# First mixer's attention taken in pairs of heads, with selection, norm and lift woven into it

## The reference, cut to what matters

```
def dsa_attention(q, k, v_lat, iq, ik, iw, w_uv):      # 8 heads of 64, top 128 keys
        dots = jnp.einsum('bqhe,bse->bqhs', iqb, ik)
        score = jnp.einsum('bqh,bqhs->bqs', iwb, jax.nn.relu(dots))
        score = jnp.where(mask, score, -jnp.inf)
        _, sel = lax.top_k(score, top_k)
...
        prob = jax.nn.softmax(logits, axis=-1)
        o_lat = jnp.einsum('bhqk,bqkl->bqhl', prob, v_sel)
        return jnp.einsum('bqhl,hld->bqhd', o_lat, w_uv)    # the lift
def diff_attention(q, k, v, lam, subln_g, lam_init):   # 4 heads, two maps each
        prob = jax.nn.softmax(jnp.where(mask, s, -jnp.inf), axis=-1)
        a = prob[0] - lam * prob[1]
...
    return rms_norm(o, subln_g) * (1.0 - lam_init)      # the heads' norm
def even_mixer(...):
    return jnp.concatenate([a_out, b_out], axis=-1) @ w_out
```

## Time and profile before

| what | before |
|---|---|
| median of 3 runs | 3308.28 us |
| lowest, highest | 3301.98, 3309.21 us |
| profiled execution, its own time | 3297.97 us |
| its span, first to last instruction | 3296.6 us |
| TensorE busy | 3149.0 us, 96% of the span |
| VectorE, ScalarE, GpSimd busy | 1364.8, 1168.3, 1147.7 us |
| mean granted TensorE clock | 0.968 |
| chain that ended last, TensorE's share | 84% |

### The profile page before, as it was taken

How to read it: one execution, slowest core, us unless ns; L and a number is a source line. 1 busy time by engine, 2 the same in 40 slices (tenths; PEclk the granted TensorE clock), 3 DMA queues, 4 the chain that set the end, 5 groups by cost and what they waited for, 6 DMA issues and landing times.

```text
span 3296.6 us, 36185 instructions
## 1 busy us (share of the span) xinstructions
PE 3149.0 (96%) x14236; PEld 2514.4 (76%) x14236; DVE 1364.8 (41%) x2455; ACT 1168.3 (35%) x2028; POOL 1147.7 (35%) x480
## 2 busy tenths in 40 slices
PE   8999998989999999999989999989999989999998
PEld 6888776668888878887758888867758768876786
DVE  5311496844121451113964321367153423156442
ACT  4222464333222442223414232344323432345422
POOL 4444431014444444444414444433314332300143
PEclk9999998799999999999999999999999999979999
DMA  4333221003333323332303333333213334300032
GB/s 141 102 96 97 81 83 39 1 26 102 96 98 98 93 89 96 98 98 89 102 21 114 97 96 101 95 97 108 86 38 97 99 104 159 96 1 1 20 96 76
DMA packets 76524, 274.33 MB, mean 83 GB/s; under 512 B 8472, under 2 KB 9368, under 8 KB 75973
## 3 DMA queue, kind: packets, MB, share of 16 engines
q1 hardware_dynamic: 76356, 272.03, 26.6%
HBM read 269.85 MB, written 2.15 MB: 83 GB/s over the span
## 4 chain that ended last, share of the span: by engine, by line
PE 84%; DVE 11%; ACT 2%; issue 2%; POOL 1%; DMA 0%; SPq 0%; ACTq 0%; DVEq 0%; POOLq 0%
PE ps L480 23%; PE ps L481 23%; PE ps L482 23%; PE ps L1479 5%; PE ps L1453 4%; DVE arena L2101 3%; PE ps L1467 1%; PE ps L1465 1%; DVE arena L1735 1%; PE ps L2671 1%; PE ps L2533 1%; POOL w_lo L455 0%; ACT w_hi L432 0%; PE ps L2484 0%; DVE arena L1724 0%
## 5 line engine op out<-in xcount | busy, mean ns | idle before, releaser
L455 POOL TENSOR_TENSOR w_lo<-ring,w_hi 128x1024 fp32r<-128x1024 f32 x463 | 1131.9, 2447 | 2123.9 <-ACT w_hi L432 2082.4
L480 PE MATMUL ps<-x_hi,w_hi 128*128 128x512 f32 x2168 | 860.3, 397 | 34.2 <-POOL w_lo L455 21.1
L481 PE MATMUL ps<-x_lo,w_hi 128*128 128x512 f32 x2168 | 849.4, 392 | 0.0
L482 PE MATMUL ps<-x_hi,w_lo 128*128 128x512 f32 x2168 | 849.1, 392 | 0.0
L432 ACT CAST w_hi<-ring 128x1024 fp32r<-128x1024 f32 x473 | 493.9, 1046 | 746.7 <-PE ps L482 741.8
L480 PEld LDWEIGHTS ps<-x_hi,w_hi 128*128 128x128 f32 x2168 | 410.7, 189 | 128.4 <-issue 19.6
L481 PEld LDWEIGHTS ps<-x_lo,w_hi 128*128 128x128 f32 x2168 | 410.6, 189 | 88.6 <-issue 4.4
L482 PEld LDWEIGHTS ps<-x_hi,w_lo 128*128 128x128 f32 x2168 | 410.4, 189 | 86.6
L480 PE MATMUL ps<-r_hi,w_hi 128*128 128x512 f32 x1120 | 437.4, 391 | 11.5 <-issue 11.5
L481 PE MATMUL ps<-r_lo,w_hi 128*128 128x512 f32 x1120 | 436.7, 390 | 0.0
L482 PE MATMUL ps<-r_hi,w_lo 128*128 128x512 f32 x1120 | 436.5, 390 | 0.0
(11 more groups left out here) (240 smaller groups left out, 3311.5 us busy)
## 6 DMA issues: line engine op xcount, KB each, us to landing
ring<-in_stream SPq DMA_DIRECT2D x473, 512.0 KB, 3.5
arena<-in_cmp_w SPq DMA_DIRECT2D x16, 512.0 KB, 4.5
arena<-frev SPq DMA_DIRECT2D x1, 3072.0 KB, 14.8
h<-in_x SPq DMA_DIRECT2D x4, 512.0 KB, 7.1
out<-arena SPq DMA_DIRECT2D x4, 512.0 KB
arena<-in_p SPq DMA_DIRECT2D x2, 512.0 KB
arena<-in_mem SPq DMA_DIRECT2D x1, 1024.0 KB
arena<-in_pool_recip SPq DMA_DIRECT2D x1, 1024.0 KB
```

The source lines that it names most:

```text
L455: self.nc.gpsimd.tensor_tensor(self.w_lo[:, n % SPLIT, :], self.ring[:, n % RING, :], self.w_hi[:, n % SPLIT, :].bitcast(F32), ALU.subtrac ...
L480: nc.tensor.matmul(out, a[0], b[0], start=start, stop=False)
L481: nc.tensor.matmul(out, a[0], b[1], start=False, stop=False)
L482: return nc.tensor.matmul(out, a[1], b[0], start=False, stop=stop)
```

## The change

`attention` is no longer used by the first mixer. In its place:

- A new function `paired_attention` takes 32 pairs: the two maps of a differential head, or two neighbouring sparse heads. The two score products of a pair lie in the upper and the lower 64 rows and follow each other directly. Its rounds are `scores(it)`, `turn(it-2)`, `values(it-4)` on TensorE; `store(it-5)` (of differential pairs), `invert(it-1)`, `bias(it)` and selection on VectorE; `store(it-5)` (of sparse pairs), `scale(it-1)`, `exponentials(it)`, `copy(it-3)` on ScalarE.
- PSUM: two banks for each of two pairs of scores, two banks for one turned pair, one bank for the output. A `turn` waits for the copy of the pair before.
- The diagonal matrices are made by ScalarE (`scale`) in place of VectorE, and one copy takes both turned units of a pair.
- The weighing of the index products moves from a stage of its own into the generator `select_keys`.
- The heads' norm (`SubNorm`) is woven into rounds 21 to 28: its sums are taken with tokens on partitions, 16 products of one column, so that root and reciprocal work on 128x16; the factors are spread back by ScalarE and a product with ones.
- The lift (`Lift`) goes by query tile, eight products of 128 columns at the end of rounds 29, 30, 32 and 36.
- `ev_out` takes its tiles in the order 4 to 7, 0 to 3, and its first two tiles are rounded at the end of the attention.

```diff
+EV_ROWS = (4, 5, 6, 7, 0, 1, 2, 3)
...
-        @block.vector
-        def _(dve):
-            k.vlink(nc.vector.tensor_copy(scores[:, 0, 0:P], k.c("chunkmask")[:, SEQ - P:SEQ]))
-            for i in range(1, TT):
-                w = P * (i + 1)
...
+def select_keys(k, dve, dots, cut, iw, scores, top):
...
+        w = P * (i + 1)
+        work = scores[:, i, 0:w]
+        for h in range(4):
+            dve.wait_ge(*cut[i, h])
+            wt = iw[:, i, h:h + 1]
+            if h == 0:
+                k.vlink(nc.vector.tensor_scalar(work, dots[i][:, h, :], wt, None, ALU.mult))
+            else:
+                k.vlink(nc.vector.scalar_tensor_tensor(work, dots[i][:, h, :], wt, work, ALU.mult, ALU.add))
+            yield i, w
+        k.vlink(nc.vector.tensor_tensor(work, work, k.c("chunkmask")[:, SEQ - w:SEQ], ALU.subtract))
+        yield i, w
         for _ in range(TOPK // 8):
             k.vlink(nc.vector.max(top, work))
             k.vlink(nc.vector.match_replace(work, top, work, gone))
...
+def paired_attention(k, pairs, scratch, turned_at, gate, steps, lift, subln, rows):
...
+            def scores(p):
+                u = pairs[p]
+                if p >= 2:
+                    pe.wait_ge(biased.handle, biased.at(2 * p - 2))
+                for j in range(2):
+                    b = 2 * (p % 2) + j
+                    if p < 2:
+                        k.bank(pe, b)
+                    ins = nc.tensor.matmul(k.ps[:, b, 0:u.w], u.q[j], u.key[j], start=True, stop=True)
+                ins.then_inc(scored.handle, 1)
+            def turn(p):
+                u = pairs[p]
+                pe.wait_ge(diag.handle, diag.at(p + 1))
+                if p >= 1:
+                    pe.wait_ge(copied.handle, copied.at(p))
+                for j in range(2):
+                    if p == 0:
+                        k.bank(pe, 4 + j)
+                    for t in range(u.i + 1):
+                        ins = nc.tensor.matmul(k.ps[:, 4 + j, t * P:(t + 1) * P], ex[p % 3][:, j, t * P:(t + 1) * P],
+                                               dg[p % 2][:, j, :], start=True, stop=True)
+                ins.then_inc(turned.handle, 1)
...
+            for it in range(n + 6):
+                if it < n:
+                    scores(it)
+                if 2 <= it < n + 2:
+                    turn(it - 2)
+                if 4 <= it < n + 4:
+                    values(it - 4)
+                subln.pe(pe, it - norm_at)
+                if it in lift_at:
+                    lift.pe(pe, lift_at[it], stored.token(last[lift_at[it]] + 1))
...
+            def bias(p):
+                u = pairs[p]
+                dve.wait_ge(scored.handle, scored.at(p + 1))
+                if p >= 3:
+                    dve.wait_ge(turned.handle, turned.at(p - 2))
+                for j in range(2):
+                    nc.vector.tensor_tensor_reduce(ex[p % 3][:, j, 0:u.w], k.ps[:, 2 * (p % 2) + j, 0:u.w], u.bias, 1.0, 3e38,
+                                                   ALU.add, ALU.min, low[:, p % 3, j:j + 1]).then_inc(biased.handle, 1)
...
+            work = steps(dve)
+            spent = 0
+            due = [weight[p] / weight[needed[TT - 1] - 1] for p in range(n)]
+            upto = np.cumsum([0] + [(5 + 2 * (TOPK // 8) + 1) * P * (i + 1) for i in range(1, TT)])
+            for it in range(n + 6):
+                if 5 <= it < joined + 5:
+                    store(it - 5)
+                if 1 <= it < n + 1:
+                    invert(it - 1)
+                if it < n:
+                    if not pairs[it].joined and pairs[it].i > 0:
+                        assert spent >= upto[pairs[it].i]
+                    bias(it)
+                    while spent < min(1.0, due[it]) * upto[-1]:
+                        spent += next(work)[1]
+                subln.dve(dve, it - norm_at)
...
+            def scale(p):
+                act.wait_ge(factor.handle, factor.at(p + 1))
+                if p >= 2:
+                    act.wait_ge(turned.handle, turned.at(p - 1))
+                for j in range(2):
+                    ins = nc.scalar.activation(dg[p % 2][:, j, :], k.c("ident"), ACT.Copy, scale=inv[:, p % 3, j:j + 1])
+                ins.then_inc(diag.handle, 1)
...
+            for it in range(n + 6):
+                if joined + 5 <= it < n + 5:
+                    store(it - 5)
+                if 1 <= it < n + 1:
+                    scale(it - 1)
+                if it < n:
+                    exponentials(it)
+                if 3 <= it < n + 3:
+                    copy(it - 3)
+                subln.act(act, it - norm_at)
+                if it == n + 3:
+                    for i in range(2):
+                        subln.applied_to(act, i)
+                        rows.round(act, i)
+                if it in lift_at:
+                    lift.act(act, lift_at[it])
+
...
+class Lift:
...
+        for h in range(8):
+            lo = 64 * (h % 2)
+            ins = k.nc.tensor.matmul(k.ps[lo:lo + 64, self.BANK, h // 2 * P:(h // 2 + 1) * P],
+                                     self.uv[:, h * 64:(h + 1) * 64], self.latent[:, h, q], start=True, stop=True)
+        ins.then_inc(self.lifted.handle, 1)
...
+class SubNorm:
...
+    def pe(self, pe, it):
+        k, nc = self.k, self.k.nc
+        if it == 0:
+            k.bank(pe, self.BANK)
+            for h in range(4):
+                pe.wait_ge(self.squared.handle, self.squared.at(h + 1))
+                for t in range(TT):
+                    ins = nc.tensor.matmul(k.ps[:, self.BANK, h * TT + t:h * TT + t + 1],
+                                           self.work[:, h, t * P:(t + 1) * P], k.c("ones")[:, 0:1], start=True, stop=True)
+            ins.then_inc(self.summed.handle, 1)
+            k.bank_read[self.BANK] = self.rooted.token(1)
+        if 3 <= it < 7:
+            h = it - 3
+            pe.wait_ge(self.spread.handle, self.spread.at(h + 1))
+            k.bank(pe, self.BANK)
+            nc.tensor.matmul(k.ps[:, self.BANK, :], k.c("ones"), self.work[:, h, :], start=True,
+                             stop=True).then_inc(self.made.handle, 1)
...
+    differential, sparse = [], []
     for i in reversed(range(TT)):
         q = slice(i * P, (i + 1) * P)
         w = P * (i + 1)
         for h in range(4):
-            for c in range(2):
-                differential.append(Unit(bq[64 * c:64 * c + 64, h, q], bk[64 * c:64 * c + 64, h, 0:w],
-                                         k.c("chunkmask")[:, SEQ - w:SEQ],
-                                         [(P, bv[:, j, h * P:(h + 1) * P]) for j in range(i + 1)],
-                                         gate=small[:, 5:6] if c else None, first=(c == 0), last=(c == 1),
-                                         dst=o[:, 4 + h, q], clamp=True))
-    attention(k, differential + sparse, scr, select_keys(k, negmask, small[:, 8:16]), in_place=False)
...
+    rows = Rows(k, "ev_out", o, [P] * KT,
+                lambda m, ps: nc.vector.tensor_tensor(k.h[:, m, :], ps, k.h[:, m, :], ALU.add), order=EV_ROWS, feed=feed)
+    paired_attention(k, differential + sparse, ex_at, turned_at, small[:, 5:6],
+                     lambda dve: select_keys(k, dve, dots, cut, iw, negmask, small[:, 8:16]), lift, subln, rows)
```

More of the change, by code:

```diff
@@ L150, in stream_plan @@
                     plan += [("ev_f", "ev_w_in", 0, "cols", EV_F), ("ev_t", "ev_w_in", 0, "tcols", EV_T),
-                             ("ev_out", "ev_w_out", 0, "rows", tiles(0, KT))]
+                             ("ev_out", "ev_w_out", 0, "rows", [tiles(0, KT)[i] for i in EV_ROWS])]
                 else:
@@ L1756, in dense_rope, with index_dots @@
     return tokens
-def index_scores(k, iq, ik, iw, scores, cut_dots, after):
+def index_dots(k, iq, ik, dots, after):
     nc, s = k.nc, k.s
-    done, cut, used = s["product_done"], s["act_step"], s["dve_read"]
-    at = {1: 0, 2: 4 * 2 * P, 3: 4 * 5 * P}
-    def dots(i, h):
-        w = P * (i + 1)
-        return cut_dots[:, at[i] + h * w:at[i] + (h + 1) * w]
+    done, cut = s["product_done"], s["act_step"]
     with Stage(nc) as block:
@@ L1824, in select_keys @@
     for i in range(1, TT):
-        work = scores[:, i, 0:P * (i + 1)]
+        w = P * (i + 1)
[10 more added lines that the diff above has]
+        yield i, w
         for _ in range(TOPK // 8):
@@ L1950, in even_mixer @@
-    for h in range(4):
-        k.bank_read[h] = copied.token(h + 5)
-        k.bank_read[4 + h] = rooted.token(h + 1)
-    for g, v in ((lifted, 8), (copied, 8), (squared, 4), (sums, 4), (rooted, 4), (used, 4)):
-        g.advance(v)
-    feed = Feed(k, "ffn2_g0")
-    rows_add(k, "ev_out", o, [P] * KT, 1.0, feed=feed).alone()
+            half = [slice(0, 64), slice(64, P)]
+            differential.append(Pair(i, [bq[c, h, q] for c in half], [bk[c, h, 0:w] for c in half],
+                                     k.c("chunkmask")[:, SEQ - w:SEQ], [bv[:, j, h * P:(h + 1) * P] for j in range(i + 1)],
```

(11 more changed lines are left out.)

249 lines of the change are left out of this document (163 added, 86 removed).

## The result

The change makes the kernel slower: 3355.15 us median (3347.34 to 3360.7, four runs) against 3305.13 (3299.68 to 3309.21, four runs), a ratio of 1.0158 with a 95% interval of 1.0143 to 1.0172. The profiled execution has a span of 3354.2 us, where before had 3296.6: 57.6 more. The first scores start at 519.0 us, as before, and the first product of `ev_out` at 773.3 in place of 707.8: 65.5 us later. So the whole loss, and 8 us more, arises inside the first attention.

What follows compares the result with a forecast made beforehand. TensorE's waits in the first attention were taken as the bound. Rounds 191, ends 8 and woven part 16 us put `ev_out` 26 us later; with 50 for the clock, 76 later: 3374 traced, 3384 by median, stated 3380 (3325 to 3418).

Steps and rivals of the forecast that it cites:

- The closed chain: First attention: scores, bias, exponentials, copy, turning, values follow in each round; 8.6 us at 512 keys against 6.06; case's chance 0.57.
- The clock: First attention: TensorE's waits make the clock swing between full and 1.2 GHz, costing 50 us.
- Take half: Clock cost set at 50 us, between nothing and 101 us for 1.2 GHz throughout the rounds.
- The full-clock term: First attention at the full clock: first product of `ev_out` at 734 us, 26 us later than 707.8.
- scores: TensorE's score products of a pair at 512 keys: between 1.3 and 2.1 us, taken as 1.5.
- the 8 us less over all rounds: If a pair's scores take 1.05 us, not 1.5, all rounds of the first attention together take some 8 us less.
- Turning and values: TensorE's eight products each at 512 keys: 1.8 us each, plus 0.2 for waking up after the wait, 3.8 in all.
- The woven part: Norm and lift inside the attention's rounds: 16 us on the chain, of it 7.2 for the lifts.
- a rival of it: Rounds of the first attention stay at the full clock: only +26 us, some 3324 to 3334; chance 0.2.
- Behind the attention: The stage from `ev_out` on keeps its 45.3 us: same slabs and products in another order.
- The sights: Signs expected in the profile after: TensorE idle ahead of turning, first bias near 519.5 us, clock 0.6 to 0.9.
- The rival "faster": Copy done before TensorE comes to the turning: `ev_out` 38 us earlier, 3260 to 3270; chance 0.06.

Runs made afterwards that it cites:

- Opened at ScalarE or at TensorE alone: Two kernels, each the change with one edit: ScalarE's copy ahead of the exponentials, 3297.8 us; TensorE's values ahead of turning, 3295.5 us.
- everything open: The change with values ahead of turning, copy ahead of diagonals and exponentials, norm and lift products between scores and turning: 3254.8 us, 0.9858 of before.
- both orders changed: The change with values ahead of turning on TensorE and copy ahead of exponentials on ScalarE: 3268.1 us, 0.9899 of before.
- the waits were filled: The change with useless products into an unused bank between scores and turning of rounds 3 to 20: 3333.6 us, 1.0103 of before.
- The nine kernels above: Follow-up kernels made from the change, without the one with norm and lift as a stage apart: medians 3254.8 to 3333.6 us.

## Why the prediction came out as it did

I gave 3380 us (3325 to 3418), slower with 0.92. Measured: 3355.

- **The closed chain** (likeliest case) is shown. I had summed a wait of 3.3 us at 512 keys down to 1.65 at 128, 79 us in 32 rounds; the trace has 84.8 ended by the copy, 10.6 of them at the start. Opened at ScalarE or at TensorE alone, half of it goes, with both all but 12.7.
- **The clock** came out as priced, 50. TensorE works 101.3 us while the clock is at 0.50, and at the full clock that takes about half: four products of values (eight instructions) stand 1.85 us at 0.50 (624.31 to 626.16) and 0.95 at 1.00 (707.26 to 708.21). So the clock costs some 50 us by this estimate, and some 48 without the first turning, behind which TensorE waits in any case. A second way agrees. The same products of turning, values, scores, sums, ones and lift are busy for 67.2 + 55.3 + 32.4 + 6.8 + 5.0 + 4.4 = 171.1 us in the change and 46.9 + 45.5 + 28.4 + 3.7 + 4.4 + 4.4 = 133.3 with everything open: 38 less, and that kernel still works 21.3 us at 0.50, 11 more to gain. "Take half" of the 101 us was a choice between two bounds, without a row for it; that it came out so closely is luck, the swing of the clock is not.
- **The full-clock term** was the one too large: 26 us, where 65.5 - 48 leaves some 17. The step that was mis-sized is the pair's **scores**, 1.5 us at 512 keys. With both orders changed a pair's scores start at 646.59 us and the values behind them at 647.65: 1.06 us. By the factor of up to two in the Trainium skill ("TensorEngine Tiling (Array Packing)", section "Theoretical Speedup") I had 1.05 as the other value; here the trace agrees with it, and it is the 8 us less over all rounds that the prediction names. My nearness to the row of alternating halves was the wrong choice. Turning and values of 512 keys took 1.86 and 1.88 us (563.09 to 564.95 to 566.83); I had 1.8 each and 0.2 for waking up after the wait. That 0.2 was no such thing: the turning of 1.09 us in the earlier trace rows had no wait ahead of it, and the 1.86 stand right behind one of 2.99.
- **The woven part** was put at 16 us; it costs 13. The total hides two errors: I left out the 16 products of one column (6.8 us at the lower clock, 3.7 with everything open), and priced four lifts at 7.2 where they took 4.4.
- The Trainium skill ("TensorE: Matmul & The Clock Gate", section "Loop structure matters more than you think") calls a loop warm in which VectorE copies a result out and the next products follow immediately. I made a rival of it for a loop whose products wait for the copy, which is not what it says. Here the clock was 0.50 for 64.8 us with waits of 1.7 to 2.9 us in each round, and 0.95 in place of 0.73 once the waits were filled. That rival had 3324 to 3334.
- **Behind the attention** I had assumed nothing. From the start of `ev_out` to the end it is 2588.8 us before and 2580.9 after, 7.9 us less. Of these 6.9 are the clock: TensorE works 110.6 us at 0.50 there before and 96.8 after. The nine kernels above with the same code in that stretch as the change took 2581.6 to 2587.1 us, so the change's own trace had a lucky one.
- **The total**: 9 us for the full-clock term, 2 for the clock, 8 for the stretch behind it, and 6 that I had put on the traced time for the median, while the change's median is that of its traced run: 3380 becomes 3355.
- **The sights**: the reciprocals of 3.35 us gone, the clock at 0.74 from 519 to 780 (0.6 to 0.9 foreseen), the copy ahead of 31 turnings (28 to 32), the woven rounds 13 us longer (under 25): as said. The first bias came at 520.8 us, not 519.5. The rival "faster" was laid on the copy's place behind the exponentials, with 3260 to 3270 for a kernel without it. The place was right, and the price for opening both chains too (3268, 3255); but moving that copy alone gives 3298, which my rival did not say.

## What to carry to other kernels

Where an engine's turn in a round waits for another engine's last step of the same round, the length of the chain is the period. Here it was paid a second time with the clock, some 48 us beside 85 of waits. Either take the producer's step ahead of the consumers of the current round, or give the waiting engine work of another round to issue. After opening one chain look for the next with the same ends: here the order of three calls in one engine's list decided 85 us of 3355 (3269.9 against 3355.2). Read every engine's order from one step back: is what it takes first already ready?

## What the runs showed that was not expected

- A product of one column is no cheaper than one of 128: 32 instructions took 6.83 us at 0.50 (0.213 each) and 3.7 with everything open (0.116), like the 0.116 of a product of 128 columns (16 in 1.86 us).
- Products into the two column halves of the array (the lift) overlap: 16 instructions in 1.09 us, 0.068 each, where 16 of full width take 1.86 (0.116 each).
- The same code takes a different time from kernel to kernel: the stretch from `ev_out` to the end took 2580.9 us in the change and up to 2587.1 in the kernels made from it, with 123.7 to 134.9 us of it at a clock of 0.50. A difference of 6 us in the whole can come from there.
